# The last stage of a two-block kernel with its operands exchanged: gated values become the loaded operand, expert rows stream past

## What is computed

```
for each of 8 heads: 16 of the 16384 experts are chosen, with softmax weights g
a   = x_normed . expert_u[e]           for the 128 chosen experts e of a token
w   = g * gelu(a)
y   = sum over e of  w * expert_v[e]
out = h + y                            (512 x 1024; h is the residual)
```

## Time and profile before

| | |
|---|---|
| median of the timed runs | 2459.72 us |
| profiled execution | 2455.8 us |
| its span, first to last instruction | 2454.1 us |
| mean granted TensorE clock | 0.977 |
| PE busy | 2374.9 us (97%) |
| DVE, ACT, POOL busy | 59%, 43%, 17% |

### The profile page before, as it was taken

One profiled execution on the slowest core, in us unless ns is written; L12 is line 12 of the kernel. 1 busy time (PEld: TensorE's weight loads), 2 busy tenths in 40 slices (PEclk: granted clock), 3 DMA queues, 4 the chain that ended last, 5 costly groups with the idle time before them and its releaser, 6 DMA issues.

```text
span 2454.1 us, 39285 instructions
## 1 busy us (share of the span) xinstructions
PE 2374.9 (97%) x14819; PEld 2100.3 (86%) x14819; DVE 1441.3 (59%) x3067; ACT 1064.9 (43%) x1958; POOL 413.4 (17%) x338
## 2 busy tenths in 40 slices
PE   6999999999999978899999999999999999999999
PEld 4888878888786456578999999999999999999998
DVE  4544444333574377442489999999977744444443
ACT  4434334222432357633344335888853332322322
POOL 0000000000200000010000101655543223333330
PEclk9999999999998789999899999999999999999999
DMA  4222322232241000022355655999999879898992
GB/s 156 94 86 78 107 88 85 86 100 88 95 171 63 1 1 1 1 94 95 94 154 161 227 173 178 388 395 385 385 373 399 324 274 355 329 346 322 343 348 87
DMA packets 131821, 462.09 MB, mean 188 GB/s; under 512 B 13840, under 2 KB 32528, under 8 KB 129888
## 3 DMA queue, kind: packets, MB, share of 16 engines
q1 hardware_dynamic: 75744, 233.87, 28.0%
q0 software_dynamic: 51440, 196.90, 21.4%
q10 hardware_dynamic: 4496, 29.36, 3.1%
HBM read 407.12 MB, written 52.43 MB: 187 GB/s over the span
## 4 chain that ended last, share of the span: by engine, by line
PE 85%; DVE 10%; ACT 3%; DMA 2%; issue 1%; POOL 0%; ACTq 0%; DVEq 0%; POOLq 0%
PE bank L428 15%; PE bank L429 15%; PE bank L430 15%; PE bank L1095 8%; PE bank L1096 7%; PE bank L1097 7%; PE bank L1063 3%; PE bank L1108 2%; DVE wlo L415 2%; PE bank L443 2%; PE bank L525 1%; PE bank L710 1%; PE bank L486 1%; ACT pair_prob L1326 1%; PE bank L729 1%; PE bank L937 1%
## 5 line engine op out<-in xcount | busy, mean ns | idle before, releaser
L428 PE MATMUL bank<-act_hi,whi 128*128 128x384 f32 (+1 forms) x1968 | 725.3, 369 | 17.0 <-DVE act_lo L1569 12.4
L415 DVE TENSOR_TENSOR wlo<-raw,whi 128x1024 fp32r<-128x1024 f32 x398 | 484.9, 1224 | 414.0 <-ACT whi L411 412.1
L429 PE MATMUL bank<-act_lo,whi 128*128 128x384 f32 (+1 forms) x1968 | 714.4, 363 | 0.0
L430 PE MATMUL bank<-act_hi,wlo 128*128 128x384 f32 (+1 forms) x1968 | 713.9, 363 | 0.0
L411 ACT ACTIVATE whi<-raw 128x1024 fp32r<-128x1024 f32 x398 | 418.2, 1055 | 457.1 <-PE bank L1097 380.3
L428 PEld LDWEIGHTS bank<-act_hi,whi 128*128 128x128 f32 x1968 | 372.1, 189 | 66.3 <-issue 20.1
L430 PEld LDWEIGHTS bank<-act_hi,wlo 128*128 128x128 f32 x1968 | 372.0, 189 | 38.1
L429 PEld LDWEIGHTS bank<-act_lo,whi 128*128 128x128 f32 x1968 | 372.6, 189 | 35.6 <-issue 0.5
L1095 PE MATMUL bank<-h_hi,whi 128*128 128x384 f32 x1024 | 349.9, 342 | 3.8 <-DVE h_lo L2200 3.8
L1096 PE MATMUL bank<-h_lo,whi 128*128 128x384 f32 x1024 | 347.6, 339 | 0.0
L1097 PE MATMUL bank<-h_hi,wlo 128*128 128x384 f32 x1024 | 345.4, 337 | 0.0
(11 more groups left out here) (354 smaller groups left out, 2679.5 us busy)
## 6 DMA issues: line engine op xcount, KB each, us to landing
raw<-tiles SPq DMA_DIRECT2D x398, 512.0 KB, 4.2
acts_dram<-gelu SPq DMA_DIRECT2D x128, 192.0 KB, 4.8
gates_dram<-stage ACTq DMA_DIRECT2D x12, 2048.0 KB, 10.5
wg<-gates_dram POOLq DMA_DIRECT2D x16, 1536.0 KB, 17.1
hf<-acts_dram POOLq DMA_DIRECT2D x16, 1536.0 KB, 12.1
bias<-alibi POOLq DMA_DIRECT2D x16, 256.0 KB, 3.0
w1s<-cmp_w POOLq DMA_DIRECT2D x1, 4096.0 KB, 13.8
res<-x_t ACTq DMA_DIRECT2D x4, 512.0 KB, 10.0
```

The source lines that it names most:

```text
L415: dve.tensor_tensor(wlo[:, j.slot, :], raw[:, j.slot, :], whi[:, j.slot, :].bitcast(F32), ALU.subtract).then_inc(lo_made, 1)
L428: pe.matmul(to, wh, x, start=(kc == 0), stop=False)
L429: pe.matmul(to, wh, xl, start=False, stop=False)
L430: last = pe.matmul(to, wl, x, start=False, stop=(kc == KC - 1))
```

## The change

The operands of the V jobs are exchanged. A job is now one expert block (n = 0 to 127): its 128 whole rows of 1024 features are the streamed operand, as two halves of 512 columns, and the loaded operand is a 128 x 128 piece of the gated values, one for each of the three token tiles. Three tiles times three products times two halves are 18 matmuls of 512 columns. The sums of the 384 tokens stand in six whole banks, with tokens on partitions, and the gathered tokens' sum in the two others (6 and 7). A quad is 2 chunks of 512 columns times 4 rows.

Blocks are weighed one a job, four jobs ahead (`V_LEAD`), in place of a group at a time. The residual is turned to tokens on partitions earlier: 8 chunks of four transposes each, after U jobs m = 11 to 14 of the first two token tiles, each chunk copied back by ACT. The restart at group 3 and `add_residual` are gone. The output is one array, stored in eight pieces; the pieces of the gathered tokens leave from job 123 on.

```diff
+V_LEAD = 4
+V_BANK = [(4, 5), (2, 3), (0, 1), (6, 7)]
+TURNS = [11, 12, 13, 14]
+OUT_FIRST = 121
-LATE = 3
...
+            def turn_residual(kc):
+                pe.wait_ge(S("x_step"), 3 + 2 * kc)
+                for tt in range(TT):
+                    last = turn(pe, bank[5][:, tt * P:(tt + 1) * P], res[:, kc, tt * P:(tt + 1) * P], ident)
+                last.then_inc(S("x_step"), 1)
+                    if tt < 2 and m in TURNS:
+                        if m == TURNS[0]:
+                            pe.wait_ge(S("routes_scaled"), 8 * tt + 16)
+                        turn_residual(4 * tt + TURNS.index(m))
...
-            def add_residual(dc):
-                return pe.matmul(bank[dc][:, mine], res[:, dc, 0:P], ident, start=False, stop=False)
+            def v_job(n):
+                j = Job(J_V + n)
                 pe.wait_ge(lo_made, j.n + 1 + RING)
...
+                pe.wait_ge(S("h_split"), n + 1)
+                slot, m = n // GJ % 2, n % GJ
+                for tt in range(TT - 1):
...
+                    t = slice(tt * P, (tt + 1) * P)
+                    hi, lo = h_hi[slot][:, m, t], h_lo[:, slot, m, t]
+                    for x, w in ((hi, whi), (hi, wlo), (lo, whi)):
+                        for half in range(2):
+                            last = pe.matmul(bank[V_BANK[tt][half]][:, :], x, w[:, j.slot, T * half:T * half + T],
+                                             start=(n == 0 and w is whi and x is hi), stop=(n == P - 1 and x is lo))
...
-                for dc in range(KC):
+                for half in range(2):
                     for j in range(4):
                         at_ = (16 * j + r % 16) * 32
-                        last = pe.matmul(bank[dc][32 * j:32 * j + 32, mine], spread[r // 16][:, at_:at_ + 32],
-                                         rows[:, (4 * r + j) % ROWS, dc, :], start=False, stop=False)
+                        last = pe.matmul(bank[V_BANK[3][half]][32 * j:32 * j + 32, :], spread[r // 16][:, at_:at_ + 32],
+                                         rows[:, (4 * r + j) % ROWS, 4 * half:4 * half + 4, :].rearrange("p k d -> p (k d)"),
+                                         start=(r == 0), stop=(r == 31))
...
+                    if tt < 2 and m in TURNS:
+                        kc = 4 * tt + TURNS.index(m)
+                        act.wait_ge(S("x_step"), 4 + 2 * kc)
+                        copy(res[:, kc, :], bank[5][:, :], S("x_step"))
...
+            for n in range(P):
+                if n + HI_AHEAD < P:
+                    make_hi(act, Job(J_V + n).ahead(HI_AHEAD))
+                if n + V_LEAD < P:
+                    weigh_hi(n + V_LEAD)
...
+            for n in range(V_LEAD):
+                weigh(0, n)
+            for n in range(V_LEAD):
+                weigh_lo(0, n)
+            for n in range(P):
+                if n + AHEAD < P:
+                    make_lo(dve, Job(J_V + n).ahead())
+                b = n + V_LEAD
+                if b < P:
+                    if b % GJ == 0:
+                        group_landed(b // GJ)
+                    weigh(b // GJ, b % GJ)
...
+                if b < P:
+                    weigh_lo(b // GJ, b % GJ)
+                if n == OUT_FIRST:
+                    dve.wait_ge(S("quads_done"), P // 4)
+                    add_up_tile(0)
+            for tile in range(1, TT):
...
+                add_up_tile(tile)
```

More of the change, by code:

```diff
@@ L1497, in weigh_hi @@
                 act.activation(h_hi[grp % 2][:, m, :], hf[:, grp % 2, m, :], ACT.Copy).then_inc(S("h_hi_made"), 1)
[L1499 to L1516, removed]
-                        act.wait_ge(S("spread_zeroed"), 2)
-                        for h in range(2):
-                            t = spread[h][:, :]
-                            diagonal = bass.AP(tensor=t.tensor, offset=t.offset + 16 * h,
-                                               ap=[list(t.ap[0]), [512, 4], [33, 16]])
-                            copy(diagonal, bank[7][:, 0:P].rearrange("p (j r) -> p j r", j=4)[:, :, 16 * h:16 * h + 16],
-                                 h0_step)
@@ L1524, in _ @@
-            act.wait_ge(S("quads_done"), P // 4)
-            for dc in range(KC):
-                act.wait_ge(S("summed"), KC + dc + 1)
-                act.dma_start(out[:, dc, :], res[:, dc, P:T]).then_inc(stored, 16)
-                copy(xtok[:, dc, :], bank[dc][:, mine], h0_step)
-            act.wait_ge(h0_step, 5 + KC)
-            act.dma_start(out_rows.rearrange("t (k d) -> t k d", k=KC), xtok).then_inc(stored, 16)
-            act.wait_ge(stored, 16 * (KC + 1))
+            for n in range(V_LEAD):
+                weigh_hi(n)
@@ L1534, in _ @@
+            for tile in range(1, TT):
+                for half in range(2):
+                    store(tile, half)
+            act.wait_ge(stored, 16 * 2 * TT)
         @block.vector
@@ new lines, in add_up_tile @@
+            def add_up_tile(tile):
+                for half in range(2):
+                    x = res[:, 4 * half:4 * half + 4, tile * P:(tile + 1) * P]
+                    dve.tensor_tensor(x, x, bank[V_BANK[tile - 1][half]][:, :].rearrange("p (k d) -> p k d", k=4), ALU.add)\
+                        .then_inc(S("summed"), 1)
+            group_landed(0)
+            for n in range(V_LEAD):
+                weigh(0, n)
+            for n in range(V_LEAD):
+                weigh_lo(0, n)
+            dve.wait_ge(S("x_step"), 3 + 2 * KC)
@@ new lines, in _ @@
+            for n in range(P):
+                if n + AHEAD < P:
[5 more added lines that the diff above has]
+                    weigh(b // GJ, b % GJ)
+                if n < V_DOTS:
+                    for _ in range(DOTS_V):
+                        dot(seen)
+                        seen += 1
+                if n == V_WEIGHTS + 1:
+                    dve.wait_ge(h0_step, 1)
+                    dve.tensor_tensor(udot[:, :], udot[:, :], w0[:, :], ALU.mult).then_inc(h0_step, 1)
+                if b < P:
[3 more added lines that the diff above has]
+                    add_up_tile(0)
@@ L2241, in _weights @@
+            for tile in range(1, TT):
+                if tile < TT - 1:
+                    dve.wait_ge(S("tiles_summed"), tile)
+                else:
+                    result_of(dve, Job(J_V + P - 1))
+                add_up_tile(tile)
 def _weights(a):
```

121 lines of the change are left out of this document (45 added, 76 removed).

## The result

The changed kernel takes 2480.36 us, median of 5 runs (2471.84 to 2482.3), against 2460.59 us (2459.43 to 2464.28) for the kernel before on the same chip: ratio 1.0078, 95% interval 1.0064 to 1.0092. By the ratio it is 19.2 us slower, where 17.0 less was forecast; the time lies some 20 us above the top of the range. The profiled execution took 2481.35 us, with a span of 2479.7.

The account below looks back on a forecast made before the run. PE was taken as the bound, its queue filling the last stage, with transfers close behind. The terms -17.6 + 0 - 1.9 - 1.9 - 1.6 + 0.7 + 6 - 0.7 summed to -17.0 us: 2442.7 us, range 2434 to 2460.

Parts of the forecast that it names:

- V jobs, -17.6: Last stage: 18 matmuls at 226.7 ns make a job 4.080 us, 0.137 less, 128 times: -17.6 us.
- rival (d): V jobs' matmul excess is not by instruction; they come out as with `mg`, or by the page's gap: 2458, chance 0.10.
- POOL's order, +6: Gathers queue behind POOL's wait to load gates; PE stalls 2.0 us at three quads: +6 us (0 to 11).
- Quads, 0: Last stage's quads: 16 records of 512 columns, strips still overlapping, keep a quad at 2.075 us: 0 us.
- Rival (b): In the quads, strips don't overlap at 512 columns: +1.68 us a quad, +54 us, 2496; chance 0.08.
- Restart and `add_residual`, -1.9: In jobs 24 to 31, `add_residual` and the restart cost PE 1.9 us, all gone: -1.9 us.
- Start, -1.9: Before V job 0, four `weigh` in place of eight stand before the first `h_lo`: PE waits 1.9 us less.
- clock in job 0, -1.6: V job 0 runs at full clock after the shorter pause: -1.6 us (0 at worst).
- Turns, +0.7: The residual's 32 transposes beside the U jobs mostly hide in PE's wait for `wlo`: +0.7 us, 3.8 without that cover.
- Per-job chain, no wait: In V jobs, DVE's 3.6 of 4.08 us and ACT's work finish in time, so PE does not wait.
- The end, -0.7: After the last additions, a 256 KB store in place of 512 KB: -0.7 us (-1.2 to +0.3).
- Rival (c): Transfers become the bound: stalls of 2 to 3 us in all 11 groups with quads, +20 to 30, 2465; chance 0.07.

Follow-up runs that it names:

- the run with four gathers: Changed kernel, POOL issuing a quad's four gathers, within a group, only when the four before have landed: 2486.92 us, ratio 1.0108.
- five jobs ahead: Changed kernel with blocks weighed five jobs ahead in place of four (V_LEAD = 5): 2450.17 us, ratio 0.9965.

## Why the prediction was wrong, step by step

- **V jobs, -17.6: wrong, a miss of 14.1.** A job takes 4.190 us, which is 128 x 0.027 = -3.5 us in place of -17.6. The step that failed is the choice of a row: between `act_hi` at 226.7 and `mg` at 233.4 ns I chose by "the streamed operand is now `whi`", and asked only where the streamed operand lies. The other bound (-2.1) was near. Both rows were explained by one fact that neither I nor the rival (d) used: `act_hi` lies in the same place as `whi` modulo 256 bytes and `mg` 128 bytes off it. An exchange of operands leaves a relative offset as it is. Nor did it help that the `h_hi` of even groups is not in the odd place at all: one load in three, `h_lo`, kept those jobs at 232.5 ns. The 0.10 for (d) was too low, since the prediction itself named the place of the loaded operand as the easiest way to fail.
- **POOL's order, +6: right in mechanism and places, wrong in size, a miss of 24.4 and the largest.** The gates leave 4.2 us after the start of the job that I named (4.0) in groups 4 and 5, 5.0 in group 13, and the three long stalls stand at the quads after jobs 37, 45 and 109. One term was mis-sized. At the five waits rows land 20.1 to 22.1 us after the gates, not 17.1: I had scaled the bytes of the earlier trace rows to four gathers. The landings in the run with four gathers show a sum instead: 11 to 13 us for the gates, shared with the weights, then 7 to 8 for the gathers, one after another. My upper bound was that sum, but with 10.8 for the gates, 18.2 in all, and I took less than it "since the queue comes in empty". The waits are then 5.4 to 6.7 us and not 2.0, and two more appear, 2.3 and 1.2 us. A second term was missing: I priced no lower clock behind these pauses, though job 0 of before had shown it, 1.6 us after a pause of 3.77; it cost 2.4 to 2.8 us three times. Together 30.4 in place of 6, where my bounds ended at 11.
- **Quads, 0: right.** 1.92 us for 16 records, and 6.23 - 4.19 = 2.04 us on the path against 2.075, which is -1.1 us for 32. Rival (b) is out. The Trainium skill (TensorE: Matmul & The Clock Gate, Part 3) has a loss of a fifth for three column strips at N = 512; here four strips show none against the short records of before.
- **Restart and `add_residual`, -1.9: consistent.** They are gone; nothing stands in their place.
- **Start, -1.9 and clock in job 0, -1.6: right in the profile after.** From the last U to the first V matmul lie 2.50 us where it was 4.11, -1.6; job 0 takes 4.27 us where it took 5.83. The second is not sure, however: in the version with the gates last the wait was 2.9 us and job 0 took 5.80.
- **Turns, +0.7: right.** Four transposes put 0.35 us between two U matmuls, eight times, 2.8 in all; the waits on `wlo` fell from 3.5 to 1.0, which leaves +0.3. From the first U matmul to the last the trace has 0.4 us more than before.
- **Per-job chain, no wait: right.** PE never waits for DVE or ACT in the stage.
- **The end, -0.7: right.** 4.8 us from PE's last start, against 5.4.
- **Rival (c), transfers as the bound:** its symptom, stalls and a lowered clock, was the nearest of all to the outcome, and 2465 its price. But its cause is out, for the last stage runs without a stall at a share of 0.92 once the gates are loaded last.

With the measured terms the sum is -3.5 - 1.1 - 1.9 - 1.6 - 1.6 + 0.3 + 30.4 - 0.6 = +20.4 us; measured was +19.2 (interval 15.7 to 22.6). The range had been cut at 2460 although (d), +15.6, and the upper bound of the stalls, +5, had the same sign and make 2463 together; the other 19 us of the stalls lay outside every bound that I had. That the price of (c) comes nearest to the time is luck: it is right in sign and not in cause.

## What to carry to other kernels

When two rows give two prices for the same instruction, find out what tells them apart before choosing one; here an edit of one word shows it, and is worth 0.3% in the old kernel and 0.6% in the new one. When a wait is moved later on a queue, list what is queued behind it and add up the landings one by one, or take them from a transfer with the same one ahead of it, rather than scale bytes; and price PE's pause with the slower matmuls that follow it. Where a load is not urgent, put it behind the urgent ones: two blocks of lines in another order were worth 27 us.

## What the hardware showed

- **The relative place of the operands.** fp32r matmuls of 512 columns start every 226.7 ns in rows in which all loaded and streamed operands lie at the same place modulo 256 bytes. With all loads 32, 64 or 128 bytes off it is 232.3 to 233.3 ns, with one load in three off 231.1 to 232.5, and with the streamed operands off 233.3 to 233.4 at 32 and 128 bytes and 229.0 at 64. At 384 columns it is 173.3 to 173.4, and 175.7 at 128 bytes. Moving all by 128 bytes changes nothing. Other offsets were not tried.
- **The distance of back-to-back matmuls.** In good places it is 13.3 ns over the columns at 2.4 GHz, at 512 (213.3) and at 384 (160.0) alike. The Trainium skill (TensorE: Matmul & The Clock Gate, Back-to-back issue gap) gives 2.5 ns over them, and no row here agrees.
- **The clock after a pause.** Waits of 5.4 to 6.7 us were each followed by work at the lower of the two levels (1.2 GHz, granted clock 0.50 behind the first), which cost 2.4 to 2.8 us. Between 2 and 3 us it went either way: after 2.17 and 2.30 us it did not fall, after 2.23 us (four gathers at a time, 0.51) and 2.9 us (start of the stage, gates last, 0.51) it did. After 1.18 us it did not.
- **Gathers behind a load.** Four gathers of 512 KB behind a load of 1.5 MB landed one after another, 1.3 to 2.5 us each, and the last of them 17.5 to 22.1 us after the load's issue, with four more behind them or not, and with the engines partly idle near the end. Where another load of 1.5 MB had left 3 us or less before the first, it was 21.1 to 24.2 us (five jobs ahead, and four gathers at a time). A gather issued when the ones before it had landed took 4.4 us (the one of 2013.78, four at a time).
